# The dense products with turned outputs: two PSUM banks per pass in place of one

## What is computed

```
h = rms_norm(x, norm_w);  split_columns(h @ w_in);  x + mixed @ w_out
h = rmsnorm(x, g);        p = h @ w_in;             x + y @ w_out
x + jnp.square(jax.nn.relu(h @ w_ff1)) @ w_ff2
proj = h @ w_in;  m = g_a * (y_a @ w_pa) + g_b * (y_b @ w_pb);  x + rms_norm_3(m @ w_o, g_post)
```

## Time and profile before

| | us |
|---|---|
| median of 3 runs | 5439.6 (5429.97 to 5440.24) |
| profiled execution, its own time | 5440.67 |
| its span | 5439.0 |
| tensor engine (matmul) busy | 4440.5 (82%) |
| tensor engine, weight loads busy | 3631.7 (67%) |
| VectorE busy | 1951.4 (36%) |
| ScalarE busy | 1324.3 (24%) |
| GpSimd busy | 963.3 (18%) |
| mean granted tensor clock | 0.886 |

### The profile page before, as it was taken

The page is one execution under the profiler, slowest core; times in us unless marked ns, Lnnn a source line. Parts: engine busy times, 40 slices in busy tenths (PEclk is TensorE's granted clock), DMA queues, the critical chain, the costliest instruction groups (busy, mean ns, idle before and its releaser), DMA issues. The chain is left out here.

```text
span 5439.0 us, 57119 instructions
## 1 busy us (share of the span) xinstructions
PE 4440.5 (82%) x21650; PEld 3631.7 (67%) x21650; DVE 1951.4 (36%) x3456; ACT 1324.3 (24%) x2232; POOL 963.3 (18%) x420
## 2 busy tenths in 40 slices
PE   6996979626786577857799997999989999888477
PEld 4885767525464466745687875788878888776355
DVE  2030666363336666522532443100023333224432
ACT  2120323121211444322100002112134444321111
POOL 1220000001130343411122221222111111122111
PEclk8997989557898798888899998999999999977688
DMA  2333011221142111021111110223133343233422
GB/s 94 102 134 85 19 25 24 63 89 44 49 145 105 59 36 30 15 80 39 43 50 45 48 47 16 97 93 139 70 104 101 91 111 90 87 120 128 117 79 84
DMA packets 275441, 407.49 MB, mean 75 GB/s; under 512 B 53381, under 2 KB 188551, under 8 KB 269579
## 3 DMA queue, kind: packets, MB, share of 16 engines
q1 hardware_dynamic: 227082, 310.93, 18.7%
q10 hardware_dynamic: 45936, 88.63, 4.3%
q0 software_dynamic: 2192, 4.80, 0.4%
HBM read 283.43 MB, written 120.85 MB: 74 GB/s over the span
## 5 line engine op out<-in xcount | busy, mean ns | idle before, releaser
L127 POOL TENSOR_TENSOR weights_wlow<-weights_raw,weights_whigh 128x1024 fp32r<-128x1024 f32 (+1 forms) x156 | 459.7, 2967 | 1966.4 <-ACT weights_whigh L118 1966.2
L220 PE MATMUL acc<-h_high_half,weights_whigh 128*128 128x512 f32 x928 | 367.4, 396 | 102.5 <-PEq L311 82.6
L220 PE MATMUL acc<-h_high_half,weights_wlow 128*128 128x512 f32 x928 | 366.2, 395 | 0.0
L220 PE MATMUL acc<-h_low_half,weights_whigh 128*128 128x512 f32 x928 | 365.5, 394 | 0.0
L118 ACT ACTIVATE weights_whigh<-weights_raw 128x1024 fp32r<-128x1024 f32 (+1 forms) x156 | 186.4, 1220 | 629.3 <-PE acc L220 203.3
L2790 PE MATMUL acc<-h_high_half,weights_whigh 128*128 128x512 f32 x768 | 332.1, 432 | 0.0
L127 POOL TENSOR_TENSOR weights_ff_wlow<-weights_ff_raw,weights_ff_whigh 128x1024 fp32r<-128x1024 f32 x72 | 176.1, 2466 | 786.0 <-ACT weights_ff_whigh L118 786.0
L223 PE MATMUL acc<-weights_whigh,h_high_half 128*128 128x512 f32 x768 | 302.7, 394 | 14.0 <-PEq L174 14.0
L2790 PE MATMUL acc<-h_low_half,weights_whigh 128*128 128x512 f32 x768 | 302.8, 394 | 0.0
L223 PE MATMUL acc<-weights_wlow,h_high_half 128*128 128x512 f32 x768 | 301.9, 393 | 0.0
L223 PE MATMUL acc<-weights_whigh,h_low_half 128*128 128x512 f32 x768 | 301.7, 393 | 0.0
(11 more groups left out here) (513 smaller groups left out, 9434.3 us busy)
## 6 DMA issues: line engine op xcount, KB each, us to landing
weights_raw<-w_cols SPq DMA_DIRECT2D x94, 512.0 KB, 5.0
weights_ff_raw<-w_ff SPq DMA_DIRECT2D x64, 512.0 KB, 3.7
weights_raw<-w_rows SPq DMA_DIRECT2D x30, 1024.0 KB, 6.3
att<-gated_result_sb SPq DMA_DIRECT2D x96, 130.0 KB, 2.2
merge_o_sb<-att SPq DMA_DIRECT2D x24, 520.0 KB, 5.5
cols<-cols1p_out ACTq DMA_DIRECT2D x40, 256.0 KB, 2.1
rows<-rows1p_out ACTq DMA_DIRECT2D x32, 256.0 KB, 2.7
x<-x_here SPq DMA_DIRECT2D x2, 4096.0 KB, 14.5
```

Source lines behind the costliest of these rows:

```text
L127: self.core.nc.gpsimd.tensor_tensor(low[p][:, hs, :], raw[half], high[p][:, hs, :].bitcast(F32), ALU.subtract).then_inc(self.core.sem("wei ...
L220: mm = nc.tensor.matmul(core.acc[b][:, :], wt[p][:, k, c * P:(c + 1) * P], h[:, k, half * HALF:(half + 1) * HALF], start=first, stop=final)
```

## The change

The transposed form takes banks two at a time. Both banks of a pair share their 128 output channels, and so the weights. For each chunk k the three kinds of product are now in the order high by whigh, low by whigh, high by wlow, and each is issued for half 0 into bank b and then for half 1 into bank b + 1. The waits for both banks stand ahead of the pair, and the two signals `product` leave with the last two matmuls of its 48. The same matmuls are issued as before, and nothing else is changed.

```
-                for b in range(nb):
+                for b in range(0, nb if transposed else 0, 2):
+
+                    pe.wait_ge(emptied[b], it + at[f"emptied_{b}"])
+                    pe.wait_ge(emptied[b + 1], it + at[f"emptied_{b + 1}"])
+                    c = b // 2
+                    for k in range(KC):
+                        for n, (h, wt) in enumerate(((high, whigh), (low, whigh), (high, wlow))):
+                            first, final = k == 0 and n == 0, k == KC - 1 and n == 2
+                            for half in range(2):
+                                mm = nc.tensor.matmul(core.acc[b + half][:, :], wt[p][:, k, c * P:(c + 1) * P],
+                                                      h[:, k, half * HALF:(half + 1) * HALF], start=first, stop=final)
+                                if final:
+                                    mm.then_inc(product[b + half], 1)
+                for b in range(0 if transposed else nb):
```

More of the change, by code:

```diff
@@ L217, in multiply @@
                             first, final = k == 0 and n == 0, k == KC - 1 and n == 2
[L218 to L223, removed]
+                            mm = nc.tensor.matmul(core.acc[b][:, 0:width], h[:, k, b * P:(b + 1) * P],
                                                       wt[p][:, k, :], start=first, stop=final)
```

## The result

The changed kernel takes 5459.78 us as the median of six runs (5453.35 to 5467.07), beside 5433.35 us for the kernel before (5429.97 to 5440.24), again six. The ratio is 1.0047, with a 95% interval of 1.0034 to 1.0060: 26 us slower. The forecast was 5460 us and slower, by 0.38%. The profiled execution took 5463.27 us, 22.6 us more than that of before, where the sum said 20.3.

The account below looks back on a forecast made before the run. Bound taken: matmul pace within calls, the last emptied bank between them. Pace and waits 0, ends 16.9 us and clock 3.4 us gave 20.3 us on 5440.7, 5461.0; the forecast was 5460 us, range 5440 to 5484.

Parts of the forecast that it names:

- the sum: Whole kernel: 16.9 us at the call ends plus 3.4 us of clock, 20.3 us slower.
- The pace: Matmuls within calls: still one per 0.227 us despite repeated weights and alternating banks; 0 us, bounds -98 and +25 us.
- The good bound: Pace when alternating banks: 0.215 us per matmul, from the norm's float32 products, 12 ns less; -98 us over 8160 matmuls.
- Rival A: Pace in mid call: repeated weights or alternating banks save 12 ns per matmul; 5395 or 5362 us, chance 0.15.
- rival C: Switches between banks: each costs 3 ns, 25 us on top, 5485 us; chance 0.08.
- Within a call they stand back to back: Matmuls inside each call: no gaps, one starting every 0.227 us in a steady stretch.
- The waits: Block start and mid block: waiting for a second bank costs 0, as it was completed at least 5.4 us earlier.
- The ends: Ends of the 19 calls: the last block's second emptying is no longer hidden; 16.9 us together.
- eight calls of one instruction: Ends of four ff2, out1, out2, proj_a0, proj_o: one more 0.69 us emptying on the path; 0.49 us each, 3.9 us.
- The clock: Restarts of the four ff2 after longer stops: lower granted clock loses 8.5 us in place of 5.1, 3.4 us more.
- The bound I gave: Clock loss at the ff2 restarts: between 0 and 5 us, around the forecast 3.4 us.
- Rival B: Whole kernel a wash: pace gains 1 to 3 ns or half the ends are hidden; 5440 to 5450 us, chance 0.14.

Follow-up runs that it names:

- third kernel: The kernel before, with the three products of a chunk in the change's order, still one bank at a time; 5437.54 us, ratio 1.0000.
- fourth kernel: The change, with one weight tile as stationary operand of all 48 products of a pair; 5463.69 us in one run.
- first kernel: The change, with the last pair of each call's last block done one bank after the other; 5436.91 us, ratio 1.0001.
- ninth kernel: The change, with all four banks done together in the last block of each four-bank call; 5573.73 us, ratio 1.0245.
- seventh: The kernel before, with 12 idle matmuls behind each of ten calls and 24 in each of four norms; 5413.86 us, ratio 0.9957.
- second kernel: The change, with only the last pair of each call paired, 19 of 170; 5468.76 us, ratio 1.0055.
- fifth: The change, with the last pair of only the four ff1 calls done one bank after the other; 5450.24 us, ratio 1.0019.
- sixth kernel: The change, with 20 more matmuls that nobody reads behind each ff1 call's last product; 5449.05 us, ratio 1.0021.
- eighth: The change, with the idle matmuls of the seventh in calls and norms, but 20 behind each ff1; 5437.96 us, ratio 0.9996.

## Why the prediction was right

**The pace: 0 forecast, 0 found.** The step from the one existing repeat in L223 to runs of four in two banks held. The third and fourth kernel show it at two, four and 48 repeats. The good bound taken from the norm's float32 products was never approached, and it rested on a misreading of the earlier trace rows. A float32 matmul of the program is two records: the norm ahead of ff1_0 issues 16 (8 chunks by 2 banks), and the profile has 32 at L358. So one takes 0.86 us and not 0.43, it changes bank at every second record only, and 0.215 us is the price of nothing in the program. Rival A is excluded by the count of matmuls, and rival C, against which the same rows were cited, by the first kernel. "Within a call they stand back to back" also has an exception: rkv2p stands still for 13.25 us behind its first block, 13.50 in the change, which the change hardly touches.

**The waits: 0 forecast, 0 found**, by the first kernel (1.0001). The ninth shows what the same two lines would have cost one block edge further on.

**The ends: 16.9 us forecast, about 15 found** in the profile after, as far as the emptyings alone go. The stops behind ff1 grew by 2.20 us (5.79 less 3.59) to 2.3 us, 9.1 us for the four (forecast 9.6). Of the eight calls of one instruction (forecast 3.9), ff2_0 to ff2_2 grew by 0.38 us each, and behind out1, out2 and proj_o the next stage's first product comes 2.89 us after the last of the call in place of 2.52, 0.37 us each: 2.2 us. The other two show nothing at the start of the next call: 71.15 us in place of 71.12 behind ff2_3, 73.41 in place of 73.53 behind proj_a0. Behind proj_a1 the next call starts 1.12 us later and behind proj_b 1.10 us, 2.2 us (forecast 2.4); behind each of cols1p, cols2p, gates2p and cols3p it is 0.33 to 0.39 us, 1.5 us (forecast 1.0).

**The clock: 3.4 us forecast, about 12 found, the term that was mis-sized.** The forecast counted the four restarts of ff2 alone. For them I took the mean of three stretches behind longer stops, 0.57. In the change all four ff2 starts are at 0.50 in their first 5 us, and the lower clock reaches beyond that window. Over the first 8 us of ff2_0 to ff2_3 the stretches of the kernel before have 28, 28, 28 and 35 matmuls:

```profile
2708.67:2716.67 8.00, 8.00 (x28) 0.79 0.40 131
...
3250.22:3258.22 8.00, 8.00 (x35) 1.00 0.40 132
```

and those of the changed kernel 23 in each, of which the first stands here:

```profile
2712.67:2720.67 8.00, 8.00 (x23) 0.62 0.39 131
```

That is 119 - 92 = 27 matmuls fewer, at 0.227 us 6.1 us. The bound I gave, +1.6 us on 3.4, was too tight, because it was read from windows that end before the slow products do.

The rest of the clock is where the forecast put nothing. Behind out1, out2 and proj_o the norm's own float32 products follow, and the 0.37 us more of stop made them slower. In the stretches, the first 5 us of these products behind out2 and behind proj_o, in the kernel before:

```profile
2574.60:2579.60 5.00, 5.00 (x12) 1.00 0.00 0
5393.61:5398.61 5.00, 5.00 (x12) 1.00 0.97 369
```

and in the changed kernel:

```profile
2574.03:2579.03 5.00, 5.00 (x8) 0.66 0.01 3
5414.50:5419.50 5.00, 5.00 (x8) 0.66 0.96 364
```

From proj_o's last product to the end of the program it is 47.92 or 47.93 us in the kernel before and in the first, third and seventh, which do not pair its last banks, and 49.99 or 50.00 in the change and in the second, fourth, fifth, sixth and eighth, which do: 2.1 us, of which 0.4 are the emptying and 1.7 the clock. Behind out2 and out1 it is 2.1 us too in the change and the second kernel, and so 5.1 us of clock for the three; but it does not come each time: behind out2 the fourth and sixth kernel lose the 0.4 us alone. rows1p, behind cols1p's longer stop, lost 1.3 us more at its restart, which may be chance, as the third kernel loses it with the stop of before. With the 6.1 of the ff2 that is 12.5 us.

Together 27.5 us, beside 22.6 between the two profiled executions and 26 between the medians, with 19 to 33 us in the interval. The two profiled executions differ by less than the terms because the stages from rows1p's last product to out1's first, which the change doesn't touch, took 808.7 us in place of 814.9. In the other traces (the ninth kernel's left out) they take 808.4 to 815.4, with and without pairs, so this is chance. The forecast had the mechanism and the size of the ends; that its sum of 20.3 stood so near the 22.6 of the profiles, and its 5460 at the very median, was in part luck. The clock term was a quarter of what it came to, and 5460 was counted from a median of 5439.6, which with six runs is 5433.35.

Rival B, a wash at 5440 to 5450, is excluded by the ratio of the change (at least 1.0034, 18 us), and the second kernel shows all of the loss with the 19 last pairs alone. Some ends were indeed hidden, those of ff2_3 and proj_a0, but not half of the sum.

## What to carry to other kernels

When two accumulators are finished together in place of one after the other, look at the last pair before a barrier: its second emptying has nothing left to hide behind. In mid loop the same pairing costs nothing as long as the banks it waits for were completed well before. Reordering products for the sake of repeated weights gains nothing where each matmul is issued with its own load and the load already lies beside the matmul ahead. And where a dense stretch follows a short stop, count the matmuls in its first 5 us: a dozen or two idle products in the stop bought back more here than any reordering of the real ones. Count the next stage's first products too, also those of a norm, where they follow the stop.

## What the runs showed of the hardware that was not expected

- Independent VectorE instructions overlap a little. The second emptying's first instruction starts 0.61 us after the instruction ahead of it (2709.00 to 2709.61), whose record is 0.69 us long; dependent ones start 0.72 us apart (2707.09 to 2707.81). Two adds take 1.29 us and four take 2.48, so one more costs 0.60 us and not 0.72. That is the overestimate at the three ff2 ends (0.49 forecast, 0.38 found). The Trainium skill (Vector Engine (DVE) Microarchitecture Reference, "5.2 Measured stream behaviour on trn2") gives, for streams of 32-bit integers, 1.0417 ns per column and about 75 ns per instruction, an estimate of 608 ns for 512 columns; the trace agrees with float32, 0.60 to 0.61 us.
- VectorE is slower beside GpSimd: in the ninth kernel's timeline the cast takes 2.53 us beside GpSimd's subtraction and 0.43 us alone (in the change's timeline, above), and the subtraction behind it 2.71 us in place of 0.69. It is so in the other traces: of the 64 casts of the four ff1, the 15 that overlap a GpSimd instruction in the kernel before take 2.50 to 2.51 us and the other 49 0.43 us. The wait of 9.6 us is made of this, two emptyings alone taking 5.1. In the change this falls on the emptying of banks 2 and 3 in mid call (one cast there takes 2.61 us), where there is time for it.
- Idle matmuls on operands at hand keep the granted clock at 1.00 across stops of 3.5 to 5.8 us, and bring it up ahead of the first real product behind a norm's longer stop. With them the first 5 us of the filled calls hold 22 matmuls in place of 12 to 15.
